# Reading back the scan's outputs: one read after the scan, or six during its last pair

## The reference

```
r, k, v = heads(lerp(0) @ w_in[0]), heads(lerp(1) @ w_in[1]), heads(lerp(2) @ w_in[2])
gate = lerp(3) @ w_in[3]
...
def step(s, inp):                       # 16 heads, two directions
    sa = jnp.einsum('dbhij,dbhj->dbhi', s, a_t)
    s = s * jnp.exp(lw_t)[..., None, :] + sa[..., None] * b_t[..., None, :] + v_t[..., None] * k_t[..., None, :]
    return s, jnp.einsum('dbhij,dbhj->dbhi', s, r_t)
...
yf = y[0] + jnp.flip(y[1], 1)
yn = ((yf - mean) * lax.rsqrt(var + GN_EPS)).reshape(B, T, D) * lnx_g + lnx_b
o = (yn + bonus.reshape(B, T, D)) * jax.nn.silu(gate)
return o @ w_out
```

## Time and profile before

| | us |
|---|---|
| median of 3 runs | 4448.01 (4444.34 to 4450.34) |
| the profiled execution | 4446.85 |
| its span | 4445.1 |
| TensorE busy | 3809.0 (86%) |
| DVE busy | 1544.3 (35%) |
| ACT busy | 1354.1 (30%) |

### The profile page before, as it was taken

How to read it: one execution, slowest core, us unless ns; L and a number is a source line. 1 busy time by engine, 2 the same in 40 slices (tenths; PEclk the granted TensorE clock), 3 DMA queues, 4 the chain that set the end, 5 groups by cost and what they waited for, 6 DMA issues and landing times. The chain is left out here.

```text
span 4445.1 us, 76078 instructions
## 1 busy us (share of the span) xinstructions
PE 3809.0 (86%) x32246; PEld 2148.3 (48%) x32246; DVE 1544.3 (35%) x3747; ACT 1354.1 (30%) x2940; POOL 206.0 (5%) x199
## 2 busy tenths in 40 slices
PE   5999577777787699999898888999959988699997
PEld 2555366666666444666466543333335455233332
DVE  2000366666676112443236531111122174211112
ACT  2000234444433122332446422222224263222221
POOL 0000000000000000010010000000012000000000
PEclk7999789989999899999999989999979999899998
DMA  5221434334444220000210049999933010899996
GB/s 206 74 92 49 130 96 120 101 106 118 121 111 114 85 106 1 20 1 23 77 59 1 1 155 334 386 395 392 399 138 94 11 39 1 293 388 393 389 391 269
DMA packets 315052, 697.62 MB, mean 157 GB/s; under 512 B 169168, under 2 KB 195920, under 8 KB 289616
## 3 DMA queue, kind: packets, MB, share of 16 engines
q1 hardware_dynamic: 293488, 613.98, 38.7%
q0 software_dynamic: 14048, 53.49, 3.4%
q10 hardware_dynamic: 7168, 25.17, 1.4%
HBM read 625.72 MB, written 64.50 MB: 155 GB/s over the span
## 5 line engine op out<-in xcount | busy, mean ns | idle before, releaser
L200 PE MATMUL ps<-arena 128*128 128x384 f32 (+8 forms) x5516 | 1599.9, 454 | 186.9 <-issue 38.7
L200 PEld LDWEIGHTS ps<-arena 128*128 128x128 f32 (+4 forms) x5516 | 917.2, 193 | 837.3 <-issue 460.6
L2635 PE MATMUL ps<-arena 128*32 128x512 f32 x9216 | 1025.7, 598 | 30.8 <-DMA arena<-in_w 26.2
L2635 PEld LDWEIGHTS ps<-arena 128*32 128x32 f32 x9216 | 305.0, 110 | 653.5 <-issue 636.5
L576 PE MATMUL ps<-arena 64*64 64x64 f32 (+1 forms) x10624 | 459.9, 240 | 179.6 <-DVE arena L1137 64.5
L576 PEld LDWEIGHTS ps<-arena 64*64 64x64 f32 x10624 | 411.0, 145 | 258.9 <-issue 101.0
L2769 DVE COPY arena<-ps 128x384 f32<-128x384 f32 x64 | 35.7, 557 | 671.0 <-PE ps L2694 671.0
L206 PE MATMUL ps<-arena 128*128 128x128 f32 x1200 | 191.7, 295 | 80.4 <-DVE arena L3083 40.7
L2745 ACT ACTIVATE arena<-ps 96x512 f32<-96x512 f32 x64 | 38.0, 593 | 625.7 <-PE ps L2635 625.7
L206 PEld LDWEIGHTS ps<-arena 128*128 128x128 f32 x1200 | 145.3, 154 | 122.2 <-DVE arena L3083 44.2
L549 DVE SCALAR_TENSOR_TENSOR arena<-arena 128x768 f32<-128x768 f32 x48 | 45.1, 1013 | 353.0 <-PE ps L200 353.0
(11 more groups left out here) (281 smaller groups left out, 3614.5 us busy)
## 6 DMA issues: line engine op xcount, KB each, us to landing
arena<-in_w SPq DMA_DIRECT2D x192, 2048.0 KB, 30.1
arena<-in_w_mod SPq DMA_DIRECT2D x24, 2048.0 KB, 9.0
arena<-in_mod_w SPq DMA_DIRECT2D x12, 2048.0 KB, 15.9
yb<-arena ACTq DMA_DIRECT2D x64, 384.0 KB, 9.9
arena<-in_rwkv_w_in SPq DMA_DIRECT2D x8, 2048.0 KB, 10.9
rkvg<-arena POOLq DMA_DIRECT2D x32, 384.0 KB, 2.6
arena<-rkvg SPq DMA_DIRECT2D x32, 384.0 KB, 3.8
arena<-di SPq DMA_DIRECT2D x192, 64.0 KB, 2.6
```

Of the source, the lines that this page charges most:

```text
L200: ins = pe.matmul(out, l, r, start=(i == 0), stop=(i == len(pairs) - 1))
L2635: return pe.matmul(bank[32 * at:32 * at + 32, :], left[:, k, 32 * g:32 * g + 32], right[:, k, :], start=first, stop=last)
```

## The change

The six outputs of pairs 0 to 5 are read back from rkvg[4] in six DMAs at beat 248 (BACK), while pair 7's scan runs. They go into tiles that are free by then: R, K, V and kk of pairs[0], last used by pair 6, and two tiles added to Recurrence. SyncE first waits for pair 6's bonus, its last products and operands, and for the six stores. The outputs of pairs 6 and 7 aren't stored any more; they stay in yf[0] and yf[1]. The projection takes a list of eight tiles in place of one tile; the other three projections get the same list form of their unchanged tile. RwkvOut no longer reads anything, over() asks for 48 in place of 64 from each of the two store semaphores, and TensorE waits for o_landed at 96.

```diff
@@ OutProj.pe
-                mm(pe, self.bank(i)[:, 0:n], [(w[:, k, j * 128:(j + 1) * 128], self.O[:, k, a:a + n]) for k in range(KT)]
+                mm(pe, self.bank(i)[:, 0:n], [(w[:, k, j * 128:(j + 1) * 128], self.O[k][:, a:a + n]) for k in range(KT)]
@@ Recurrence
+    BACK = 248
@@ Recurrence.__init__
+        q = self.pairs[0]
+        self.O = [q.R, q.K, q.V, q.kk, K.take(T), K.take(T), *self.yf]
@@ Recurrence.sp
-                if e == 9:
+                if e == 9 and m < 6:
                     sp.wait_ge(self.tlv.sem, self.tlv.at(m, "out"))
                     sp.dma_start(K.scr["rkvg"][4, m], self.yf[m % 2]).then_inc(s[f"o_stored{m % 2}"], 16)
...
+            if t == self.BACK:
+                sp.wait_ge(self.bnv.sem, self.bnv.at(6, "bonus1"))
+                sp.wait_ge(self.prm.sem, self.prm.at(41, "vt"))
+                sp.wait_ge(self.opv.sem, self.opv.at(41, "akc"))
+                for i in range(2):
+                    sp.wait_ge(s[f"o_stored{i}"], 48)
+                for m in range(6):
+                    sp.dma_start(self.O[m], K.scr["rkvg"][4, m]).then_inc(s["o_landed"], 16)
             if (due := self.mod_due(t)) and due[1] == 0 and due[0] < 29:
@@ Recurrence.over
-        e.wait_ge(s["o_stored0"], 64)
-        e.wait_ge(s["o_stored1"], 64)
+        e.wait_ge(s["o_stored0"], 48)
+        e.wait_ge(s["o_stored1"], 48)
@@ RwkvOut
-        K.top = into.inner
-        self.O = K.take(KT, T)
-        self.proj = OutProj(K, "rwkv", K.I["rwkv_w_out"], self.O, K.MODS[0], 16, ((0, 0, TX), (1, TX, TC)),
+        self.proj = OutProj(K, "rwkv", K.I["rwkv_w_out"], rec.O, K.MODS[0], 16, ((0, 0, TX), (1, TX, TC)),
                             ((rec.opm.sem, 48), (K.s["mod_sums"], 30)))
 
     def sp(self, sp):
         self.proj.sp(sp)
-        self.rec.over(sp)
-        sp.dma_start(self.O, self.K.scr["rkvg"][4].rearrange("k p t -> p k t")).then_inc(self.s["o_landed"], 16)
 
     def pe(self, pe, sums):
         self.rec.over(pe)
-        pe.wait_ge(self.s["o_landed"], 16)
+        pe.wait_ge(self.s["o_landed"], 96)
```

More of the change, by code:

```diff
@@ L1815, in __init__ @@
         self.O = K.take(KT, TX)
-        self.proj = OutProj(K, "mla", K.I["mla_w_out"], self.O, K.MODS[1], 16, ((0, 0, TX),),
+        self.proj = OutProj(K, "mla", K.I["mla_w_out"], [self.O[:, k, :] for k in range(KT)], K.MODS[1], 16, ((0, 0, TX),),
                             ((heads.mm, heads.mm_at(7, "q")), (heads.mm, heads.mm_at(15, "q"))), first=3)
@@ L2311, in __init__ @@
         self.K, self.heads = K, heads
-        self.proj = OutProj(K, "ab", K.I["w_out_ab"], heads.O, K.MODS[2], 16, ((0, 0, TX), (1, TX, TC)), ((K.s["ab_mm"], 32), (K.s["ab_mm"], 32)))
+        self.proj = OutProj(K, "ab", K.I["w_out_ab"], [heads.O[:, k, :] for k in range(KT)], K.MODS[2], 16, ((0, 0, TX), (1, TX, TC)), ((K.s["ab_mm"], 32), (K.s["ab_mm"], 32)))
     def sp(self, sp):
@@ L2578, in __init__ @@
         free = (K.s["c_mm"], 36)
-        self.proj = OutProj(K, "c", K.I["w_out_c"], self.O, K.MODS[3], 16, ((0, 0, TX),), (free, free))
+        self.proj = OutProj(K, "c", K.I["w_out_c"], [self.O[:, k, :] for k in range(KT)], K.MODS[3], 16, ((0, 0, TX),), (free, free))
     def sp(self, sp):
```

## The result

The changed kernel takes 4425.69 us (median of 6 runs, 4417.72 to 4435.57), the kernel before 4446.18 (6 runs, 4440.33 to 4455.18). The ratio is 0.9944, with a 95% interval of 0.9928 to 0.9961: 17 to 32 us less, by the medians 20.5. A second series gave 4426.43 (8 runs) against 4446.67 (11 runs), ratio 0.9953 (0.9940 to 0.9966), 15 to 27 us less.

A forecast was written before the change was run, and what follows sets the result against it. It took the bound to be late transfers between the last output and the projection, inside TensorE's 30.0 us wait. 4446.85 - 22.1 + 0 = 4424.75, or 4425.9 from the median; predicted 4425.5, range 4419 to 4433.

The forecast's parts named there:

- The joint's sum: Between the scan's last output and its output projection: projection starts at 1474.1 in place of 1496.24, gain 22.1 us.
- What was late next: At the projection's start: TensorE waits for DVE's last output, then passes some six counters that stand already, 0.3 us.
- The cold start: Start of the projection at half clock: 1.7 us lost before and after the change, 1.7 either way in the range.
- The six loads: Output reads at beat 248, ahead of modulation weights and et stores: cost 0, bounds no gain and 3 us.
- The sum: Whole kernel: 4424.75 from the profiled execution, 4425.9 from the median of three runs; predicted 4425.5, between the two.
- The scatter: Spread of whole-kernel runs: 3 us either way allowed within the range of 4419 to 4433.
- The scan pays 3 to 8 us: Rival, scan from beat 248: slacks of 1 us and an in-order queue make loads cost 3 to 8 us; chance 0.08.
- The weights are late next: Rival at the joint: SyncE still held until the last output, only 9 to 14.5 us won, about 4436; chance 0.05.
- The clock stays low: Rival in the projection: half clock throughout, 82 us more, 4508; chance 0.02, shared with anything else making it slower.

The follow-up runs named there:

- e3: Changed kernel with six more 384 KB stores of X to unread scratch rows right behind the six loads of beat 248; one run, 4428.22 us.
- e2: Changed kernel with SyncE issuing the two halves of w_out only after the last output is written; one run, 4438.54 us.
- e4: Changed kernel with eight extra matmuls of unused result on TensorE between the last variance matmuls and the wait for the last output; one run, 4412.72 us.
- after: The first profiled execution of the changed kernel, set against the kernel before; this execution took 4417.72 us.
- e0: The changed kernel profiled once more, no edit; this execution took 4422.73 us, ratio to the kernel before 0.9953.
- e5: Changed kernel with the six loads at beat 284 in place of 248, the only edit; one run, 4427.54 us.
- e6: Changed kernel with the six loads at beat 284 and four projection groups begun (k = 0 to 6) before the last output; 4414.59 us, ratio to before 0.9933.

## Why the prediction was right, point by point

- **The joint's sum was right, and for its reasons.** Forecast 22.1 us of gain, measured in the joint 22.45 - 0.05 = 22.40. I had taken 0.3 us for TensorE to pass its row of counters; it took 0.05 for all of them together. The range of this term, 21.6 to 22.4, just holds it.
- **What was late next** was as said: w_out's issues lie at 1432.5 and behind the sums of 1438.95, and DVE's output ends the wait. Each half of the change was tried alone (9.7 and 13.9 us).
- **The cold start** stays, as forecast. Against the 8.84 us of before the first group took 0.3 us less to 1.0 more in the four traces with the pause of 7.6 us, inside the 1.7 allowed.
- **The six loads** were put at 0, bounds 0 and 3. They cost 0.3 to 1.6 us. The slack of about 1 us was mis-sized on both sides. The weights left 3.6 us behind the start of the sums of beat 248 (1366.31 - 1362.75), where 2.8 were forecast, because the six issues took 3.77 us and not 2.8; and they landed 12.3 us after their issue, where 10.3 to 11.0 were (1368.1 to 1379.1 at the latest). Together that is 2.1 to 2.8 us late. That TensorE waited only 0.27 us, from 1378.51, is luck: its own sums of beat 248 had run at half clock and made it 1.0 us later. The Trainium skill (DMA: Bandwidth & Descriptors, "Queues, rings and completion order") states that descriptors on each DMA engine are consumed in ring order, and the traces agree: the small stores behind the loads landed after 4.7 to 5.5 us, and in the kernel before, where the weights ahead of them had all but landed, after 2.2 to 2.4. The figure of 358 GB/s that the same page of the Trainium skill has under "Bandwidth" was passed again: 409 GB/s in e3, from 1371 to 1375 us.
- **The sum** is then 22.4 us, less 0.3 to 1.6 for the loads, and less 1.0 to plus 0.3 for the cold start: 20 to 22 us, and the medians say 20.5 and 20.2. That the forecast, 4425.5, lies 0.2 from the median is luck in part: the runs spread over 18 us, and the median of before, 4448.01 over three runs when the forecast was made, is 4446.18 over six. From this one the same 22.1 us give 4424.1, which is 1.6 too low, about what the loads and the cold start cost.
- **The scatter was taken too small.** I allowed 3 us either way from three runs of before. The traces reach beat 248 up to 11.4 us apart, ahead of anything that the change does. The unchanged stages behind the projection differ by up to 13.5 us from trace to trace, and within the scan, from beat 254 to the last output, it took 93.2 to 94.3 us in four traces and 97.6 to 99.3 in the five others. In those five the last pair's mean and variance matmuls ran at half clock (2.90 us in place of 1.53 each); that is 2.7 us of it, the rest wasn't traced further. The time range of 4419 to 4433 holds both medians, but not every run.
- **The rivals.** "The scan pays 3 to 8 us": with these bytes it paid 0.3 to 1.6; with twice the bytes it was 9 to 10.5 more (e3). "The weights are late next" was built (e2) and costs 8.5 us, at the short end of the 7.9 to 13.6 named. "The clock stays low": in each of the traces in which it had fallen it rose again 2.9 to 5.5 us behind the projection's start (e4, which kept it up, apart).

## What to carry to other kernels

A DMA that waits for the last result of a stage holds up everything issued behind it on its engine; look for the loads queued there that need nothing of that result, for they are as much of the pause as the result's own round trip (here 8.5 to 9.7 of 22.4 us). Bulk moved into a latency-bound loop is cheap only up to the slack of the small transfers behind it, and then costs about its transfer time (7.6 us of wait in e3) and the clock that falls in the pause; the issues alone take time too, for six of them held the loads behind them on SyncE for 3.8 to 4.5 us; put it behind the last of them if the data isn't needed sooner. When a wait shrinks from a transfer to a short pause, ask whether a sum can be begun without its last term: here that shortened the way from the variance matmuls to the last add by 7 to 8 us.

## What the runs showed of the hardware that was not expected

The clock differs between executions by more than I had allowed: at beat 248 the same modulation sums took 1.92 us or 2.89 to 3.29, the same variance matmuls 1.53 or 2.90, from one execution to the next, at granted clocks of 1 and 0.5. This is not tied to the loads, since e6 had none there and was slow (3.29), and e2 and e4 had them and were not. A pause of 7.6 us cost 1.7 us more in the next eight matmuls (sixteen records, e3), one of 7.6 ahead of the projection 1.4 to 2.7 us (e4 against after, e0, e3 and e5). How soon the clock came back behind that pause differed as well: after 5.5, 4.7, 3.4 and 2.9 us of the projection (after, e0, e3, e5); what decides this was not tested. And the waits on six counters and on the weights, of which only the one for the last output was open, cost TensorE no more than 0.05 us together.
